# One Trainium2 core, an encoder layer with routed experts: fills of empty slots moved, and transposes of the identity in TensorE's waits between the last projection tile and the first expert

## The reference, cut to what matters

```python
h = rmsnorm(xp, g_mix[l])
rq, rk, rv, rg, dq, dk, dv, gr, gd = project(h, w_in[l], pos_p, g_q[l], g_k[l])
o_r, s_fin = retention_prompt(rq, rk, rv, log_gamma)
o_d = diff_attn_prompt(dq, dk, dv, lam)
xp = gated_merge(xp, retention_out(o_r, rg, g_ret[l], w_ret_o[l]),
                 diff_out(o_d, g_sub[l], lam_init, w_diff_o[l], xp.dtype), gr, gd, w_out[l])
xp = xp + hier_moe(rmsnorm(xp, g_ffn[l]), w_group[l], b_group[l], w_expert[l], b_expert[l],
                   w_gate[l], w_up[l], w_down[l])
...
g_idx = jnp.argmax(g_logits, axis=-1)
top_v, top_i = lax.top_k(e_prob, TOP_K)
combine = jnp.sum(jax.nn.one_hot(global_idx, N_EXPERTS, dtype=F32) * (g_w * top_v)[..., None], axis=1)
for e in range(N_EXPERTS):
    he = jax.nn.silu(xt @ w_gate[e]) * (xt @ w_up[e])
    y = y + combine[:, e:e + 1] * (he @ w_down[e]).astype(F32)
```

## Time and profile before

| what | us |
|---|---|
| median of 3 runs | 1140.6 (1140.55 to 1144.69) |
| the profiled execution, its span | 1142.49, 1140.7 |
| TensorE, VectorE, ScalarE, GpSimd busy | 1036.9 (91%), 647.5 (57%), 514.1 (45%), 155.1 (14%) |
| chain that ended last | PE 81%, DMA 10%, DVE 3%, ACT 2%, issue 2% |
| waits of TensorE after the last projection tile | 0.68, 5.35, 4.11, 1.75, 11.33, 1.40 |
| granted clock, 802 to 824 and 826 to 832 | 0.50 (1.2 GHz) |
| start to start of 128x512 products at the full clock, 834 to 838 | 0.235 |
| load of the first expert's rows, issue to landing | 3.68 |

### The profile page before, as it was taken

One profiled execution on the slowest core, in us unless ns is written; L12 is line 12 of the kernel. 1 busy time (PEld: TensorE's weight loads), 2 busy tenths in 40 slices (PEclk: granted clock), 3 DMA queues, 4 the chain that ended last, 5 costly groups with the idle time before them and its releaser, 6 DMA issues.

```text
span 1140.7 us, 12143 instructions
## 1 busy us (share of the span) xinstructions
PE 1036.9 (91%) x4736; PEld 835.2 (73%) x4736; DVE 647.5 (57%) x897; ACT 514.1 (45%) x690; POOL 155.1 (14%) x179
## 2 busy tenths in 40 slices
PE   4979399999999999999999999999299999999993
PEld 3767378787777776777787788787178888888882
DVE  4645367514443444333343754767688888988870
ACT  3521123333443434432335031345458787877851
POOL 1000002011021020111013000001202121212111
PEclk9999799999999999999999999999599999999997
DMA  9253445545245161344146454225799999999962
GB/s 309 71 199 148 168 164 188 169 166 198 86 161 168 64 232 48 127 141 152 57 168 226 173 184 148 74 82 179 267 415 366 377 406 385 400 390 390 400 232 40
DMA packets 59890, 237.31 MB, mean 208 GB/s; under 512 B 5328, under 2 KB 5504, under 8 KB 47216
## 3 DMA queue, kind: packets, MB, share of 16 engines
q1 hardware_dynamic: 39088, 162.25, 37.2%
q0 software_dynamic: 20736, 74.19, 20.1%
HBM read 199.05 MB, written 47.09 MB: 216 GB/s over the span
## 4 chain that ended last, share of the span: by engine, by line
PE 81%; DMA 10%; DVE 3%; ACT 2%; issue 2%; POOL 1%; SPq 0%; ACTq 0%; DVEq 0%; POOLq 0%
PE ps L441 20%; PE ps L443 20%; PE ps L442 20%; DMA raw<-in_w_in 7%; PE ps L1608 3%; PE ps L1609 3%; PE ps L1624 2%; PE ps L1584 2%; DMA q_tok<-z_q 2%; PE ps L1758 2%; PE ps L1661 1%; PE ps L1869 1%; PE ps L1690 1%; PE ps L1741 1%; PE ps L1772 1%
## 5 line engine op out<-in xcount | busy, mean ns | idle before, releaser
L441 PE MATMUL ps<-w_hi,s_hi 128*128 128x512 f32 x672 | 272.4, 405 | 29.0 <-issue 27.7
L442 PE MATMUL ps<-w_hi,s_lo 128*128 128x512 f32 x672 | 264.6, 394 | 0.0
L443 PE MATMUL ps<-w_lo,s_hi 128*128 128x512 f32 x672 | 264.5, 394 | 0.0
L441 PEld LDWEIGHTS ps<-w_hi,s_hi 128*128 128x128 f32 x672 | 128.1, 191 | 58.3 <-issue 30.0
L395 DVE TENSOR_TENSOR w_lo<-raw,w_hi 128x2048 fp32r<-128x2048 f32 x42 | 96.2, 2290 | 97.6 <-ACT w_hi L390 97.4
L443 PEld LDWEIGHTS ps<-w_lo,s_hi 128*128 128x128 f32 x672 | 127.9, 190 | 27.5
L442 PEld LDWEIGHTS ps<-w_hi,s_lo 128*128 128x128 f32 x672 | 128.2, 191 | 26.8 <-issue 1.0
L848 ACT ACTIVATE stage<-ps,x_rstd 128x512 f32<-128x512 f32 x64 | 44.0, 689 | 198.8 <-PE ps L443 198.8
L390 ACT CAST w_hi<-raw 128x2048 fp32r<-128x2048 f32 x42 | 80.0, 1908 | 66.3 <-DMA raw<-in_w_in 61.1
L751 POOL DMA_INDIRECT out_y<-y_exp,s_idx x16 | 45.9, 2869 | 231.7 <-ACT y_exp L1069 231.7
L413 DVE TENSOR_TENSOR lo_x<-raw_x,w_hi 128x2048 fp32r<-128x2048 f32 x32 | 71.9, 2284 | 3.8 <-ACT w_hi L408 3.8
(11 more groups left out here) (282 smaller groups left out, 1759.4 us busy)
## 6 DMA issues: line engine op xcount, KB each, us to landing
raw<-in_w_in SPq DMA_DIRECT2D x32, 1024.0 KB, 8.1
raw_x<-in_w_up SPq DMA_DIRECT2D x30, 1024.0 KB, 12.2
raw_x<-in_w_down SPq DMA_DIRECT2D x18, 1024.0 KB, 12.3
raw<-in_w_gate SPq DMA_DIRECT2D x16, 1024.0 KB, 11.2
raw_x<-in_w_gate SPq DMA_DIRECT2D x16, 1024.0 KB, 12.8
raw<-in_w_down SPq DMA_DIRECT2D x14, 1024.0 KB, 10.8
x_slots<-in_c_empty SPq DMA_DIRECT2D x4, 2112.0 KB
x_exp<-x_slots POOLq DMA_DIRECT2D x16, 528.0 KB, 13.0
```

The costliest lines, as they stand in the source:

```text
L441: nc.tensor.matmul(out, s_h, w_h, start=first, stop=False)
L442: nc.tensor.matmul(out, s_l, w_h, start=False, stop=False)
L443: return nc.tensor.matmul(out, s_h, w_l, start=False, stop=last)
```

## The change

Three things. The fills on SyncE's queue move from blocks 4 to 8 to blocks 32 to 36, the sink rows of y with them. TensorE gets `keep_busy`: it transposes the identity onto itself into product bank 0, 150 times in six places, after a wait that the last copy but one out of the banks is done. On ScalarE and VectorE the splits of the expert's blocks 2 and 3 come one tile earlier, VectorE scales a tile's rows before its choice in place of after it, and it splits blocks 4 and 5 only when all scatters have landed.

```diff
--- before.py
+++ after.py
@@ -505,15 +505,16 @@
         load_x(2)
         load_x(3)
         sp.dma_start(x_tok[0:SAMPLE, PT, :], a["x_sample"][0]).then_inc(x_in[PT], 16)
-        sp.dma_start(y_dram[SINK:SINK + P, :], a["c_empty"][:, 0:D_MODEL]).then_inc(y_init, 16)
         for n in range(2, N0):
             dense_load(n)
-            if 4 <= n < 4 + NG:
-                e = EPG * (n - 4)
+            g = n - BPC * IN_CHUNKS
+            if 0 <= g < NG:
+                e = EPG * g
                 sp.dma_start(x_slots[e * CAP:(e + EPG) * CAP, :].rearrange("(e c) x -> e c x", e=EPG)[:, 0:P, :],
                              a["c_empty"].unsqueeze(0).to_broadcast([EPG, P, XW])).then_inc(slots_empty, 16)
-            elif n == 4 + NG:
+            elif g == NG:
                 sp.dma_start(x_slots[PAD:PAD + P, :], a["c_empty"]).then_inc(slots_empty, 16)
+                sp.dma_start(y_dram[SINK:SINK + P, :], a["c_empty"][:, 0:D_MODEL]).then_inc(y_init, 16)
 
         def expert_load(j, i, q, e, kind, part):
 
@@ -1032,8 +1033,8 @@
             if t == PT:
                 lower_half_of(4)
                 lower_half_of(5)
-            if n >= 3:
-                split_hi(act, 0, 0, n - 1)
+            if n in (2, 3):
+                split_hi(act, 0, 0, n)
             if n:
                 exps(ORDER[n - 1])
         source_hi(4, ORDER[PT])
@@ -1475,20 +1476,17 @@
             evacuate_out(4, t)
             if n:
                 root_of_tile(ORDER[n - 1])
+                rows_of_tile(ORDER[n - 1])
                 choose(ORDER[n - 1])
             evacuate_out(5, t)
-            if n:
-                rows_of_tile(ORDER[n - 1])
-            if n >= 3:
-                split_lo(dve, 0, 0, n - 1)
+            if n in (2, 3):
+                split_lo(dve, 0, 0, n)
         place_rows(ORDER[PT - 1])
         source_lo(4, ORDER[PT])
         root_of_tile(ORDER[PT])
         rows_of_tile(ORDER[PT])
         choose(ORDER[PT])
         place_rows(ORDER[PT])
-        split_lo(dve, 0, 0, 4)
-        split_lo(dve, 0, 0, 5)
 
         dve.wait_ge(pos_ready, TT + 1)
         totals = ps[:, 7, TT * NE:(TT + 1) * NE]
@@ -1499,6 +1497,10 @@
         v.tensor_scalar(npass[0:1, 0:1], cmax[0:1, 5:6], 1.0, None, ALU.add).then_inc(npass_ready, 1)
         own(v.tensor_scalar(left[:, :], totals, pad_row, float(PAD), ALU.subtract, ALU.add))
         own(v.tensor_scalar(slot_row[:, :], base16, -float(PAD), None, ALU.add))
+
+        dve.wait_ge(dispatched, 16 * 2 * TT)
+        split_lo(dve, 0, 0, 4)
+        split_lo(dve, 0, 0, 5)
 
         def next_slots():
 
@@ -1846,10 +1848,19 @@
             if n:
                 logits(ORDER[n - 1])
             dense(3, IN_CHUNKS + 5, t, p_ready)
+        def keep_busy(times):
+            pe.wait_ge(p_evacuated, TT * OUT_CHUNKS - 1)
+            for _ in range(times):
+                transpose(ps[:, 0, 0:P], ident, ident)
+
         positions(PT - 1)
+        keep_busy(6)
         next_source(5, ORDER[PT])
+        keep_busy(10)
         logits(ORDER[PT])
+        keep_busy(32)
         positions(PT)
+        keep_busy(15)
         pe.wait_ge(row_ready, TT)
         for s in range(TT):
             last = mm(ps[:, 7, TT * NE:(TT + 1) * NE], ones16[:, :], sel[:, s, :], start=s == 0, stop=s == TT - 1)
@@ -1906,7 +1917,11 @@
         def expert_pass(j):
             e0 = NE * j
             first = isinstance(j, int)
+            if first:
+                keep_busy(75)
             rows_in(j, 0, first)
+            if first:
+                keep_busy(12)
             up_gate(j, 0, e0, 2, first)
             rows_in(j, 1)
 
```

## The result

The changed kernel takes 1153.04 us (median of 6 runs, 1149.52 to 1153.6) against 1141.16 of the kernel before (6 runs, 1139.87 to 1144.69); the ratio is 1.009 with a 95% interval of 1.0074 to 1.0106. The profiled execution has a span of 1151.0 us, 10.3 more than before. The forecast of 1130 with its range of 1107 to 1147 did not hold; the rival in which the z_rg loads fall behind the fourth fill had given 1153.8.

The account below looks back on a forecast made before the run. The prediction took TensorE, busy nine tenths of the span, as the bound, so only its stalls or half-clock stretches could give time. Terms: -33.15+32-4.2-2.5-3.0 = -10.9 us, median 1129.7, forecast 1130, range 1107 to 1147.

Parts of the forecast that it names:

- the rival in which the z_rg loads fall behind the fourth fill: Late place: second z_rg load lands behind the fourth fill, 24 us more, 1153.8 us; chance 0.12.
- Term 1: Projections, chunks 2 and 3: weight loads no longer queue behind the fills; gain 33.15 us.
- Term 2: Chunks 15 to 17: the moved fills delay weight and gate loads, above all z_rg; cost 32 us.
- Term 3: Router's last tile: its choice starts earlier after VectorE's work is reordered; gain 4.2 us.
- Term 4: GpSimd's last two scatters run faster without VectorE's two splits beside them; gain 2.5 us.
- Term 5: Router into first expert: transposes hold TensorE's full clock, speeding row transposes and first 11 products; gain 3.0 us.
- my rival on the clock: Router into expert: transposes don't hold the clock, 32 take 7.9 us, expert starts 9.1 later, 1148.6 us; chance 0.08.

Follow-up runs that it names:

- e4: Changed kernel, each late fill in two transfers of half rows, still 4 outermost groups, packets of 2112 bytes: 1151.2 us, ratio 1.009.
- e7: e5 without the 150 transposes of `keep_busy`: 1103.0 us, ratio 0.967 to the kernel before.
- e11: e5 with the second expert's two gate block loads (2 MB) held until the first experts' rows have landed: 1104.2 us, ratio 0.966.
- e5: Changed kernel with fills written 128 rows outermost and back at blocks 4 to 8: 1103.8 us, ratio 0.967 to the kernel before.
- e10: e5 with VectorE's splits of blocks 4 and 5 ahead of the totals again, not waiting for the scatters: 1104.0 us, ratio 0.966.
- e1: Changed kernel with the fills back in their early place, blocks 4 to 8: 1135.8 us, ratio 0.996 to the kernel before.
- e2: Kernel before with only the fills moved to blocks 32 to 36: 1157.2 us, ratio 1.014.
- e12: Kernel before with only the form of its fills changed, 128 rows outermost: 1108.8 us, ratio 0.970.
- e8: e5 with 110 transposes in place of 75 ahead of the first expert's rows: 1102.7 us, ratio 0.967 to the kernel before.

## Why the prediction was wrong, point by point

**Term 1, the fills leave the early place: right.** 33.15 foretold, 33.60 measured at the end of chunk 3. One reading in it was off by a little: the 0.27 us in the earlier trace rows are ScalarE's wait for TensorE, so chunk 3 ended at 161.67 and not at 161.40, and the term should have been 33.4.

**Term 2, they arrive at chunk 15: the step that failed.** 32 foretold, 50.5 measured. (The 50.5 is what is left over at t0; read directly, VectorE's second gating comes 648.15 - (630.19 - 33.6) = 51.6 us later than without the fills.) The first steps held: the load behind the first fill, the stall of 8 us in chunk 15 (7.54), and the load behind the third fill, which was split from 631.31 in the changed kernel against 628 foretold. What failed is "The third fill with its load: 24.05 and two z_rg loads, 6.8: about 661.9". It charges a gate load by its bytes at the rate of all 16 engines, 3.4 us, and lets it be through when the weight load in front of it is. The runs show turns: a gate load has 20 packets on each engine, and beside a fill each of them waits for one of 49 KB, 2.0 us for a pair. So the third fill let some ten through on each engine and the weight load behind it some thirty; the second z_rg load was not done when the fourth fill began and came after some ten turns more, 50 us after its issue. The median of the two was 39.5 us; with packets of 2 KB in the fill (e4) 13.1. But e4 shows too that long turns are not the whole cost: with short ones the weight load came 8.7 us later and the time stayed. The sum let gate loads and weight load be through together; on these 4 engines what the one gained the other lost. A second thing that it left out: the stall in chunk 15 moves GpSimd's issue of z_rg as well, to 597.22 where 618.01 - 33.6 = 584.4 would have been its time. What of the 18.5 us is due to this no run separates. I had the right worry, that all hangs on how "the slow engines serve the two queues", but looked for a proportion other than one to one. It was one to one, in packets of twelve times the size. The z_q store of the earlier trace rows, which I held against the rival, didn't tell this, as the fill was nearly over when it was issued.

The rival "The z_rg loads fall behind the fourth fill" (chance 0.12, 1153.8) is what happened, for the second of the two loads, and for another reason than the one I gave it: not less than one turn for each of SyncE's, but too small a turn. The forecast that it gives, 1153.8 against 1153.0 measured, is near by luck in part: its 56 us for term 2 were 5.5 too many, and the 9.7 of terms 3 to 5 were 3.1 too many the other way. Its price of 24 us more was 18.5.

**Term 3, the router's last tile: right.** The positions of the last tile start at 823.14, 10.6 us after t0, against 14.8 before: 4.2, as foretold. Without the transposes (e7) it is 11.0, so 3.8 of the 4.2 are the new order of VectorE's work.

**Term 4, the scatters: right in its place, but it lies on a path with another wait.** 0.95 and 0.95 us in place of 2.47 and 1.90. But what the expert waits for is that they land. The rows' load is issued 833.91 - 812.54 = 21.4 us after t0 against 820.41 - 795.61 = 24.8 before, 3.4 us earlier and not 6.7. Terms 3 and 4 bring the scatters forward into the time in which the second expert's weights fill the engines (DMA share 0.75 from 826 to 834, 0.42 from 811 to 820.5 in the kernel before). e11 shows these loads as the cause in e5. By the Trainium skill, SBUF — State Buffer, section Who interferes with whom, as the prediction drew on it, this term would be nothing. That does not fit e10: beside two `tensor_tensor` splits the scatters took 2.48 and 1.89 us, without them 0.95. The prediction used half of that section: it also says that a VectorE instruction with two inputs in SBUF holds up a GpSimd instruction that reads SBUF. The splits have two such inputs; whether this is what happens to the scatters no run here shows.

**Term 5, the clock: right in its mechanism, over-sized.** In the changed kernel the clock is 1.00 from 818 to 834, where TensorE does little but transposes, and in e1 it rose under them. The Trainium skill's rule (TensorE: Matmul & The Clock Gate, Part 4: PE-mode transpose) that such transposes don't count as busy does not fit this. But e1 shows too that a fall just ahead of them is paid by the work queued behind: 32 cost 6.58 us, as my rival on the clock had it (7.9). 3.0 us were foretold; e7 against e5 gives 0.6 at the 25th product, of which the products themselves give 1.8, and the later start takes 1.2 back. At the wait of 3.99 us in front of the rows the clock fell after all (8 transposes in 1.88 us); I had put that wait at under 1 us, because I had the rows landing 3.3 us earlier.

Terms 3 to 5 together: the 25th product starts 34.75 us after t0 against 39.74, 5.0 us and not 9.7. The rest of the 6.6 comes at the very end: behind the same wait of 2.09 us the last products run at a clock of 0.76 in the kernel before and at 1.00 in the changed one. All four kernels without the transposes (the one before, e2, e7 and e12) end at 0.76, nine with them at 1.00, and e8, with 110 for 75, at 0.76. So a part of the transposes in it is neither shown nor excluded, and what decides it stays open.

```profile
1117.00:1124.00 7.00, 6.29 (x20) 5.00 (x21) 0.65 (x1) 0.00 (x0) 1.45 (x1) 0.76 0.48 80
```

```profile
1129.00:1136.00 7.00, 5.86 (x24) 4.43 (x24) 0.62 (x1) 0.44 (x1) 1.42 (x1) 1.00 0.50 80
```

**The sum**: -33.6 + 50.5 - 6.6 = +10.3, the difference of the two spans. With 50.5 for term 2 and the other terms as foretold the sum would have been +7.7, and the forecast 1148.

**Best version.** e5, e7, e8, e10 and e11 cannot be told apart: 1103 to 1104 us, 3.3% faster than the kernel before. About 34 of the 37 us come from the form of the fills (e12: 1142.5 to 1108.8).

## What to carry to other kernels

Before moving a transfer that is in the way, ask why it takes so long: this one used 4 of 16 engines because its outermost dimension was 4, and two edited lines were worth more than any place that was tried for it. Where two queues meet on an engine, count turns, not bytes: a load of short packets beside one of long packets is slowed by the length of the other's packet, and shortening those only changes who is last. A gain on an engine is worth what the next wait leaves of it: the scatters' 2.5 us came down to some half a us, and 3.6 us won at the start of the expert were gone 16 us later.

## What I had not expected of the hardware

One packet of the fill moves 49 KB, and while it runs nothing else gets through on its engine: 12 packets of either queue in 6 us on 4 engines. VectorE's splits lengthen GpSimd's scatters by nearly the same amount each time, 2.47 and 1.90 us, 2.48 and 1.89 in e10, against 0.95. And the granted clock at the end of a kernel was 0.76 in five kernels and 1.00 in nine, behind the same wait of 2.09 us; what decides it these runs do not show.
